# Key products of the last seven of sixteen cached-key items: from VectorE to GpSimd, in halves

## The reference, cut to what matters

```python
# decoding part of moba_attention: 8 queries, 8 heads of 64, 8 pages of 128 cached tokens each
s = jnp.einsum('bhqd,bhnkd->bhqnk', q_c, kg, preferred_element_type=jnp.float32) * scale
gate = jnp.einsum('bhqd,bhnd->bhqn', qh, kmean)       # picks the key blocks
# pool_mixer: trailing-window means of the prompt's channels, minus the channels themselves
diffs.append(wsum / cnt - uf[..., sl])
```

## Time and profile before

| | |
|---|---|
| median of 3 runs | 603.79 us (603.11 to 609.97) |
| the profiled execution | 604.71 us, its span on the core 603.0 us |
| mean granted TensorE clock | 0.952 of full speed |
| busy, share of the span | PE 90%, DVE 58%, ACT 28%, POOL 7% |

### The profile page before, as it was taken

The page is one execution under the profiler, slowest core; times in us unless marked ns, Lnnn a source line. Parts: engine busy times, 40 slices in busy tenths (PEclk is TensorE's granted clock), DMA queues, the critical chain, the costliest instruction groups (busy, mean ns, idle before and its releaser), DMA issues.

```text
span 603.0 us, 10197 instructions
## 1 busy us (share of the span) xinstructions
PE 541.0 (90%) x3917; PEld 445.9 (74%) x3917; DVE 347.3 (58%) x541; ACT 168.2 (28%) x235; POOL 44.2 (7%) x107
## 2 busy tenths in 40 slices
PE   4759999998899898988879789987999999999997
PEld 2428678576578776667554139876999999999996
DVE  1046276658688897956655536475565466454441
ACT  2310110632122223321000215253433434334331
POOL 7300000000102910000011000000000000000000
PEclk9888989989689999999989889997999999999999
DMA  5997338356129485725639998594546645545201
GB/s 196 304 344 241 91 120 279 117 127 221 60 70 302 140 264 167 253 78 203 208 90 386 365 359 290 161 289 156 181 152 198 197 153 191 171 162 192 72 20 37
DMA packets 99437, 114.68 MB, mean 190 GB/s; under 512 B 7343, under 2 KB 82240, under 8 KB 99372
## 3 DMA queue, kind: packets, MB, share of 16 engines
q1 hardware_dynamic: 93368, 104.46, 54.2%
q10 hardware_dynamic: 5188, 7.67, 3.8%
q0 software_dynamic: 832, 1.89, 0.8%
HBM read 111.20 MB, written 2.97 MB: 189 GB/s over the span
## 4 chain that ended last, share of the span: by engine, by line
PE 69%; DVE 16%; DMA 6%; ACT 4%; issue 3%; ACTq 1%; SPq 1%; DVEq 0%
PE bank L335 65%; DVE prod L917 3%; DVE s_all L1013 3%; DMA ring<-in_ada_w_dram 2%; DVE mats L917 2%; DMA ring<-in_w_out_dram 2%; DMA ring<-in_cache_v_dram 1%; DVE cv L1121 1%; DVE BTP L917 1%; PE bank L387 1%; PE bank L358 1%; ACT w_part L1704 1%; DMA prod<-in_dn_norm_w_dram 1%; ACT adaS L1536 1%; PE bank L518 1%
## 5 line engine op out<-in xcount | busy, mean ns | idle before, releaser
L335 PE MATMUL bank<-a_hi,w_part 128*128 128x264 f32 x832 | 154.5, 287 | 2.1 <-DVE a_lo L1458 2.1
L917 DVE TENSOR_TENSOR w_part<-ring,w_part 128x2048 fp32r<-128x2048 f32 (+1 forms) x38 | 84.9, 2236 | 90.8 <-ACT w_part L1704 90.8
L335 PEld LDWEIGHTS bank<-a_hi,w_part 128*128 128x128 f32 x832 | 130.8, 191 | 2.6 <-issue 2.6
L335 PE MATMUL bank<-a_lo,w_part 128*128 128x264 f32 x416 | 119.0, 286 | 0.0
L1704 ACT ACTIVATE w_part<-ring 128x2048 fp32r<-128x2048 f32 (+1 forms) x38 | 70.9, 1869 | 86.8 <-PE bank L335 75.4
L335 PE MATMUL bank<-hT,ring 128*128 128x264 f32 x352 | 87.4, 411 | 4.1 <-ACT proj L1559 2.1
L335 PEld LDWEIGHTS bank<-hT,ring 128*128 128x128 f32 x352 | 71.0, 204 | 20.2 <-issue 7.4
L335 PEld LDWEIGHTS bank<-a_lo,w_part 128*128 128x128 f32 x416 | 79.6, 191 | 0.1
L335 PE MATMUL bank<-hid_hi,w_part 128*128 128x264 f32 x352 | 64.9, 285 | 0.0
L335 PEld LDWEIGHTS bank<-hid_hi,w_part 128*128 128x128 f32 x352 | 54.6, 188 | 0.1
L335 PE MATMUL bank<-hid_lo,w_part 128*128 128x264 f32 x176 | 49.7, 283 | 0.0
(11 more groups left out here) (321 smaller groups left out, 569.6 us busy)
## 6 DMA issues: line engine op xcount, KB each, us to landing
ring<-in_ada_w_dram SPq DMA_DIRECT2D x24, 1024.0 KB, 7.1
ring<-in_cache_k_dram SPq DMA_DIRECT2D x64, 256.0 KB, 3.6
ring<-in_w_in_dram SPq DMA_DIRECT2D x11, 1024.0 KB, 6.0
ring<-in_w_gate_dram SPq DMA_DIRECT2D x11, 1024.0 KB, 5.3
ring<-in_w_up_dram SPq DMA_DIRECT2D x11, 1024.0 KB, 5.3
ring<-in_cache_v_dram SPq DMA_DIRECT2D x40, 256.0 KB, 4.1
ring<-in_w_down_dram SPq DMA_DIRECT2D x8, 1024.0 KB, 5.3
ring<-in_cache_v_dram ACTq DMA_DIRECT2D x24, 256.0 KB, 4.8
```

Source lines behind the costliest of these rows:

```text
L335: return pe.matmul(out, lhsT, rhs, start=start, stop=stop, skip_group_check=True)
L917: return v.tensor_tensor(out, a, b_, op)
```

## The change

The products of items 9 to 15 (`SHARED = 9` is the first) are made by GpSimd, each as two halves of 128x1024. VectorE only sums them, a half at a time. A half of `prod` may be written again when VectorE has summed it (`k_reduced`), and it may be summed when GpSimd has written it (`k_products`). The ring's slot is released by GpSimd's second half. GpSimd now follows `ORDER` too, and its other work is put between the products.

```diff
--- before.py
+++ after.py
...
+    SHARED = 9
...
-        released, singles = {}, {"pe_read": 0, "keys_read": 0, "w_split": 0, "part_read": 0}
+        released, singles = {}, {"pe_read": 0, "keys_read": 0, "k_products": 0, "w_split": 0, "part_read": 0}
...
             def k_item(q, hf):
 
-                slot = arrived(v, ("k", (q, hf)))
-                v.wait_ge(sem("qb"), q + 1)
-                ins = tt(prod[:, :].rearrange("p (k n) -> p k n", k=PGI), slot.rearrange("p (k n) -> p k n", k=PGI),
-                         bc(qb[:, q % 2:q % 2 + 1, :], [P, PGI, AW]), ALU.mult)
-                used_up(ins, ("k", (q, hf)), "keys_read")
-                v.wait_ge(*released[("k", (q, hf))])
-                o = (q * NPG + hf * PGI) * H
-                ins = v.tensor_reduce(s_all[:, o:o + PGI * H], prod[:, :].rearrange("p (g d) -> p g d", d=HD), AX, ALU.add)
+                n = HALVES * q + hf
+                if n < SHARED:
+                    slot = arrived(v, ("k", (q, hf)))
+                    v.wait_ge(sem("qb"), q + 1)
+                    ins = tt(prod[:, :].rearrange("p (k n) -> p k n", k=PGI), slot.rearrange("p (k n) -> p k n", k=PGI),
+                             bc(qb[:, q % 2:q % 2 + 1, :], [P, PGI, AW]), ALU.mult)
+                    used_up(ins, ("k", (q, hf)), "keys_read")
+                    v.wait_ge(*released[("k", (q, hf))])
+                    o = (q * NPG + hf * PGI) * H
+                    inc(v.tensor_reduce(s_all[:, o:o + PGI * H], prod[:, :].rearrange("p (g d) -> p g d", d=HD), AX, ALU.add),
+                        "k_summed")
+                    v.wait_ge(sem("k_summed"), n + 1)
+                else:
+                    for w in range(2):
+                        m = 2 * (n - SHARED) + w
+                        v.wait_ge(sem("k_products"), m + 1)
+                        o = (2 * n + w) * (PGI // 2) * H
+                        inc(v.tensor_reduce(s_all[:, o:o + PGI // 2 * H],
+                                            prod[:, 1024 * w:1024 * w + 1024].rearrange("p (g d) -> p g d", d=HD), AX, ALU.add),
+                            "k_reduced")
+                    v.wait_ge(sem("k_reduced"), 2 * (n - SHARED) + 2)
                 if hf == HALVES - 1:
-                    ins.then_inc(sem("k_scored"), 1)
-                    v.wait_ge(sem("k_scored"), q + 1)
-                else:
-                    step(ins)
+                    v.sem_inc(sem("k_scored"), 1)
 
...
+            def key_products(n):
+
+                q, hf = n // HALVES, n % HALVES
+                if n < SHARED:
+                    return
+                item = ("k", (q, hf))
+                slot = arrived(g, item)
+                g.wait_ge(sem("qb"), q + 1)
+                if n == SHARED:
+                    g.wait_ge(sem("k_summed"), SHARED)
+                for w in range(2):
+                    m = 2 * (n - SHARED) + w
+                    if m >= 2:
+                        g.wait_ge(sem("k_reduced"), m - 1)
+                    ins = g.tensor_tensor(prod[:, 1024 * w:1024 * w + 1024].rearrange("p (k n) -> p k n", k=PGI // 2),
+                                          slot[:, 1024 * w:1024 * w + 1024].rearrange("p (k n) -> p k n", k=PGI // 2),
+                                          qb[:, q % 2:q % 2 + 1, :].to_broadcast([P, PGI // 2, AW]), ALU.mult)
+                    used_up(ins, item, "k_products")
+
+            def decayed_queries(_):
...
+            def key_stores(_):
...
+            def value_stores(_):
...
-            for c in range(PCH):
+            def pooled(c):
+                g.wait_ge(sem("proj_out"), out_count(PCH - 1))
+                g.wait_ge(sem("rcnt_made"), 1)
+                g.wait_ge(sem("cT_made"), 1)
                 src, at = proj[:, c, 0:T], 0
                 w = 1
...
+                if c == PCH - 1:
+                    g.sem_inc(sem("pool_prompt_done"), 1)
...
+            def tail_stores(_):
...
+            go = {("KK", 0): decayed_queries, ("M", 1): key_stores, ("TAILS", 0): value_stores, ("H", 0): lambda _: pooled(0),
+                  ("L", 5): lambda _: pooled(1), ("H", 5): tail_stores}
+            for st, n in ORDER:
+                if st == "K":
+                    key_products(n)
+                elif (st, n) in go:
+                    go[st, n](n)
```

More of the change, by code:

```diff
@@ L1855, in _ @@
             outs[0] += 2
[L1857 to L1876, removed]
@@ L1877, in _ @@
-            g.wait_ge(sem("cT_made"), 1)
+            def key_products(n):
[15 more added lines that the diff above has]
+                    used_up(ins, item, "k_products")
@@ new lines, in decayed_queries @@
+            def decayed_queries(_):
+                g.wait_ge(sem("ebc"), 1)
+                g.wait_ge(sem("qk_d"), 1)
+                ebc = w_a
+                for h in range(GH):
+                    c, r = h // 2, slice(64 * (h % 2), 64 * (h % 2) + 64)
+                    step(g.tensor_tensor(qdT[r, c, :], cv[r, c, P:T], ebc[r, h * P:(h + 1) * P], ALU.mult))
+                g.sem_inc(sem("qdT"), 1)
+            def key_stores(_):
+                g.wait_ge(sem("k_rows"), 2)
+                for r in range(TT):
+                    g.dma_start(k_prompt[0, 0, r * P:(r + 1) * P].rearrange("t h d -> t (h d)"), stg[:, r, :])\
+                     .then_inc(sem("krow_out"), 16)
@@ L1879, in add_back @@
+            def value_stores(_):
+                g.wait_ge(sem("v_rows"), 2)
+                for r in range(TT):
+                    store(v_prompt[0, 0, r * P:(r + 1) * P].rearrange("t h d -> t (h d)"), vnat[:, r, :])
+                g.wait_ge(sem("k_rows8"), 1)
+                g.wait_ge(sem("v_rows8"), 1)
+                store(k_sample[0, :, 0].rearrange("q h d -> q (h d)"), nat8[:, 1, :])
+                store(v_sample[0, :, 0].rearrange("q h d -> q (h d)"), nat8[:, 2, :])
             def add_back(dst, src, d):
```

9 lines of the change are left out of this document (4 added, 5 removed).

## The result

The changed kernel takes 613.79 us (median of 15 runs, 609.07 to 618.19). The kernel before, run beside it, takes 607.22 (15 runs, 603.11 to 609.97), which is 3.4 us more than the three runs that the prediction started from. The ratio is 1.0104, with a 95% interval of 1.0079 to 1.013: slower by 1%, where 605.0 us had been forecast. The ratios leave out a run that is more than 1.5% above the fastest of its kernel (none of these fifteen, but two of twelve in `e1`, three of twelve each in `e4` and `e7`, and one in `e16` that took 1792.39 us), while the medians are of all runs. The profiled execution took 610.77 us, its span is 609.0 us at a mean granted clock of 0.948; before it was 604.71, 603.0 and 0.952.

A forecast was written before the change was run, and what follows sets the result against it. VectorE and TensorE were taken as both nearly full in the changed stretch, GpSimd as having room. Lateness of 4.0 us less recovered waits of 1.7 and 1.1 gave +1.2 on 603.8, so 605.0 us, range 597 to 612.

The forecast's parts named there:

- A: The forecast: the SBUF lock passes to and fro between GpSimd's halves and VectorE's maskings; 605.0 us, chance 0.45.
- C: Rival: GpSimd keeps the lock through both halves, the first masking waits 3.5 us, the second none; 611.4 us, chance 0.2.
- B: Rival: GpSimd gives way and VectorE hardly waits, so the whole ceiling is won; 598.2 us, chance 0.2.
- D: Rival: GpSimd's products come late and hold up VectorE's sums; 609 us if five items each wait 1 us, chance 0.1.
- M1: First M stage beside GpSimd's products: its two maskings wait 1.7 and 0.8 us, VectorE is +2.5 us late.
- M2: Second M stage: first masking starts 3.0 us late, the second adds 0.8, VectorE is +3.8 us late.
- M3: Third M stage: loses 2.0 us more, leaving VectorE, and TensorE's transposition behind it, +3.7 us late.
- the transposition at 233.13: TensorE behind the fourth M stage, where it waited at 228.21 before: VectorE's lateness of +4.0 us passes to it in full.
- 4.0 - 1.7 - 1.1 = +1.2: Last sum: TensorE's 4.0 us lateness, less its vanished waits at the pooled channels (1.7) and at 278.05 (1.1).
- K14 and K15: Last two items: K14 wins VectorE 2.1 us; with K15's help TensorE's waits of 1.66 and 1.06 us go.
- I let it move as a whole: Cached values and matrix products behind 313 us: shifted by whatever TensorE gains or loses up to 283 us, length unchanged.
- The ceiling: TensorE's waits for VectorE from 193 to 296 us: a faster VectorE can give back 2.8 + 1.7 + 1.1 = 5.6 us.

The follow-up runs named there:

- e1: Changed kernel with all sixteen products back on VectorE, GpSimd's other work left in its new order: 609.29 us, ratio 1.0004.
- e4: Changed kernel with all products on VectorE and, in their places on GpSimd, four idle 128x1024 memsets an item: 610.27 us, ratio 1.0033.
- e7: Changed kernel with idle fill matmuls on TensorE at five places where it waits for VectorE: 608.5 us, ratio 1.0008, mean clock 0.949.
- e16: Changed kernel with each product made in four GpSimd instructions of 128x512 instead of two of 128x1024: 608.02 us, ratio 1.0013.
- e12: Changed kernel with the products of the last two items, K14 and K15, given back to VectorE: 612.77 us, ratio 1.0111.
- e13: Changed kernel as it is, profiled again to see where the clock falls: 609.38 us at mean clock 0.943.
- e15: Changed kernel as it is, a further profile to see where the clock falls: 609.23 us at mean clock 0.946.
- e10: Kernel before the change, with the same fill matmuls as e7: 610.01 us, ratio 1.0045, mean clock 0.948.
- e9: Changed kernel with each product made in eight GpSimd instructions of 128x256 instead of two of 128x1024: 605.19 us, ratio 0.9978.
- e2: Changed kernel without the last seven items' products, GpSimd only counting its semaphore up, decoding output wrong: 600.09 us, ratio 0.9885.

## Why the prediction was wrong

**Right.** The mechanism of the forecast (A) is the one that runs. A half takes 2.35 us where 2.39 was reckoned, an undisturbed pair 4.68 (4.8), a half sum 1.21 (1.22). The lock passes to VectorE between two GpSimd instructions that follow one another: C would have shown 3.5 us and nothing on the maskings, the trace has 2.47 and 1.20. B is out by the same rows, D too: no sum waits for a product. The pooling is done at 224.7 us and needed at 267.48, and with the stores it costs nothing that `e1`'s ratio shows. The time is within 2% of before, on the slow side, as forecast. Read as lateness against before, less the 1.2 to 1.4 us that were there from the start, and with up to 1.2 us of it perhaps the order's (`e1`), the ledger stood up to the first heads: M1 +2.0 (+2.5 forecast), M2 +3.0 (+3.8), M3 +2.4 (+3.7), the transposition at 233.13 +3.7 (+4.0), 0.3 to 1.3 less than forecast.

**Wrong, the last term: "4.0 - 1.7 - 1.1 = +1.2".** It counted on VectorE being ahead by then and TensorE's waits at 261.94 and 278.05 going. The second is gone, the first is still there, 1.27 at 267.48, and a wait of 0.99 has appeared at 259.21, where there was none. These two waits follow a VectorE instruction that a product held up, K14's by 1.1 us and K15's by 1.55. I had priced blocking for the maskings alone, and had given K14 and K15 a gain with no price: 2.8 us in the sum, 0.8 by the stretches with and without their products on GpSimd (129.9 and `e12`'s 130.7). The rule that the prediction cites covers the `TENSOR_SCALAR` as well, on the same page and in the same section of the Trainium skill (its `tensor_scalar` contends in the modes that use both ports); I took from it only the part on two inputs. The profile's lateness at the first cached values is +2.9 after all, net of the start, in place of +1.2: 2.7 us by the stretch. That is 1.5 us of the miss.

**Not priced at all: the clock.** "I let it move as a whole" stood for everything behind the stretch, and a granted clock that TensorE's waits lower stood at nothing in the sum. Within the runs of one kernel, 0.01 of mean clock goes with 3.0 us (after) and with 2.6 to 4.2 (before, by group of runs; 3.0 over all 88). The 0.0116 between the means of 0.9481 and 0.9365 is then about 3.5 us (3 to 5 by the extremes) of the 6.2 by which the mean times of the two fifteens (607.1 and 613.3) differ, and some 2.7 remain, as much as the stretch has in the first profile. This is an estimate from what goes together over the runs, not a measurement of a cause. For it speak the windows of `e13` to `e15`, which show the fall in the places of the longer waits, and the fill of `e7`, which brings the clock back and 0.6 to 1% of the time with it without shortening the path, while `e10` shows no such gain for the kernel before. Against it, the three profiles with a fall are no slower as a whole than the two without, and `e12`, with the same waits, has none. That TensorE's longer waits bring the fall about is thus supported, not shown; which of the filled waits it takes was not tried.

**The base.** The three runs given had a median of 603.79, the fifteen 607.22: 3.4 us of the distance from 605.0 to 613.79 is that, and belongs to no mechanism. The remaining 5.4 are 1.5 of the missing recovery, about 3.5 of clock by the estimate above, and 0.4 that I can't assign. That they nearly add up is partly luck, as the stretch behind the first cached value, 289.9 us before and 291.8 after, is 290.0 in `e1`, 292.3 in `e9` and 290.8 in `e12`, and so varies by as much as those microseconds from one execution to the next. The range, 597 to 612, ended 1.8 us too low: more than that is the base, and nothing in it stood for the clock.

**The ceiling** was 5.6 us by the waits and 7 by `e2` (1.15%). Halves lose all of it and 1% more, eighths keep 0.2% of it, which is not told apart from nothing.

## What to carry to other kernels

Work for GpSimd that reads SBUF is not free because GpSimd idles: count every VectorE instruction with two SBUF inputs, or of a two-port form, that can fall beside it, and price each at what is left of one GpSimd instruction. Where the other engine can't be avoided, cut the GpSimd instruction short before moving it: moving it behind the maskings cost another 1%, cutting it into eighths won 1.3%, and the lowest median lay where the products just came in time. A few microseconds of TensorE waits in small pieces may cost the same again in the granted clock, so look at the clock of many runs, not at the one profile.

## What the runs showed that was not expected

- Small VectorE instructions are the worst neighbours: a 128x36 addition went from 0.20 to 1.90 us and a 128x16 one from 0.17 to 1.72, since the wait is GpSimd's length and not their own.
- A GpSimd product costs 2.34 us for 1024 columns and 0.8 for 256: four short ones take 36% longer than one long one, and sixteenths, at 0.52, nearly double an item (8.36 against 4.68 us).
- In the profile after, every one of the ten maskings ends 0.54 to 0.57 us behind the end of a GpSimd half: it was served when GpSimd's present instruction ended. In five of them the second half was ready to follow, and came behind the masking.
